# The stick-breaking loop taken by pairs of heads, with the softplus split into a high and a low half for its suffix sums

## The chip, the cores and the metric

One Trainium2 chip, one core. The time is device microseconds of one execution of the whole program. Three executions of the kernel before took 3491.86, 3499.81 and 3503.06 us. The engines are named as in the profile: PE is TensorE (PEld its weight loads), DVE is VectorE, ACT is ScalarE, POOL is GpSimd, SP is SyncE, which only issues DMAs here.

## What is computed

Sequence 512, width 1024, fp32 throughout. Two layers of a first block (`DEPTH = 2`), each with two SwiGLU feed-forwards, a mixer and a gated embedding; then a block with a sparse attention ("dsa"), and one with dilated attention ("dil"), each with a feed-forward. The mixer of the first block has three branches; this case is about the first.

```python
def stick_breaking_attention(q, k, v):          # 4 heads of 64, blocks of 128 queries
    z = einsum("bqhd,bkhd->bhqk", q[:, start:end], k[:, :end]) * scale
    mask = s_idx < t_idx                        # key before query
    log_not = where(mask, -softplus(z), 0.0)
    after = cumsum(log_not, axis=3, reverse=True) - log_not
    w = where(mask, exp(log_sigmoid(z) + after), 0.0)
    out = einsum("bhqk,bkhd->bqhd", w, v[:, :end])

def latent_attention(c_q, c_kv, ...):           # 8 heads
    q = rmsnorm(c_q, g_q) @ w_uq                # 8 pieces of weights give q, k and v of all heads
    kv = rmsnorm(c_kv, g_kv) @ w_ukv
    ...
```

## The kernel before

Everything is kept transposed: channels or keys on the 128 partitions, the 512 tokens along the free axis. Each matmul with weights is done in three: the weights are split by POOL into a high half `WH` and a low half `WL` of type fp32r, the activations likewise by ACT (`HH`) and DVE (`HL`), and PE adds high by high, low by high and high by low (L566 to L568, function `piece`). SP loads the weight pieces into a ring of slots as PE releases them (`piece_used`), POOL splits them (L490, L492), PE waits on `w_split`. Matmuls without weights take fp32 operands directly; PE runs each of them as two instructions.

Engines run their own lists in order and wait for each other by semaphores; nothing is reordered. In each of the two layers the mixer begins with `project_mix` (18 pieces), then runs `stick_breaking_and_latent_heads`, a loop over the 16 units `SB_UNITS` (4 heads by 4 blocks of keys, last block first), then `attend("mla")`.

A unit (h, b) has keys of block b in the partitions and the S - 128 b queries from that block on in the free axis, so its width is 128, 256, 384 or 512. Its steps:

- PE `z(u)`: scores by one fp32 matmul over 64 rows (L776), and the strict mask by a bf16 matmul (L777), into one of four banks of PSUM, one for each block, `psA` and `psB`.
- ACT `log1p(u)`: Abs, Exp, Ln (L1307, L1309, L1311) into `SBE`, each after the one before.
- DVE `softplus(u)`: max(z, 0) + log1p in one instruction (L1610) into `SBL`, fp32.
- PE `r(u)`: for each block k from b to 3, adds -softplus, by fp32 matmuls with a triangle (`tri`) or minus ones (`onen`) (L784), onto z in the same bank.
- ACT `weight(u)`: Exp of the bank (L1318) into `SBW`.
- PE `pv(h)`, when the four blocks of a head are there: four fp32 matmuls with 64 columns of values (L792) into half of the partitions of `psD`.

`r(u)` and `weight(u)` run `LATE = 2` units behind `z(u)`. Between the units lie the eight weight pieces of the latent attention, `latent_pieces(m)` at every second unit, 15 matmuls of 512 columns for m = 0, 1, 2, 3, 5, 7 and 6 for m = 4, 6, into `psC`. DVE scales their results (L1619 to L1624) and adds one to `mla_done`; PE waits for that before it takes `psC` again. `turn_latents(c)` rotates queries by one fp32 matmul (L820, c = 0, 1 only) and transposes four blocks of values (L823). DVE finishes the rotation, ACT copies the values (L1333).

The mean of the squares of the residual stream, needed for the scale `RS` of each normed stage, is one fp32 matmul with `onen`, `mean_square_x` (L622), which stands behind the fifth piece of the stage; ACT turns it into `RS`, and DVE needs `RS` for each projection that it takes out of PSUM.

In the "dsa" block `project_dsa` takes 18 pieces; the keys and queries of an index branch are rotated (`rotate`, L851, and `turn` on DVE, L1672 to L1675), its weights transposed (`index_weights`, L1029), and 24 logit matmuls (`logits`, L1021) feed a long top-k selection on DVE.

Of the kernel before, what the change touches and what calls it, by code (L numbers as in the profile page):

```python
# [117 lines left out]
def program(nc, A, trips):  # L118
# [86 lines left out]
    SBE = sb("SBE", [P, 3, S], offset=Yo)  # L205
    SBL = sb("SBL", [P, 10 * P], offset=Yo + 6 * KB)
    SBW = sb("SBW", [P, 10 * P], offset=Yo + 11 * KB)
# [39 lines left out]
    z_ready, zl_ready, zsp_ready, e_ready, w_ready = map(sem, ("z_ready", "zl_ready", "zsp_ready", "e_ready", "w_ready"))  # L247
# [92 lines left out]
    INDEX, MEMORY_ROUNDS = 8, 10  # L340
    logit_bank = lambda i: (PB, PC)[i % 4 // 2][:, i % 2]
# [77 lines left out]
    LATE = 2  # L419
# [132 lines left out]
    def _(pe):  # L552
# [66 lines left out]

        def mean_square_x():  # L620
            pe.wait_ge(xsum_ready, n.full(xsum_ready))
            pe.matmul(MS_X, onen, Y[:, 0], start=True, stop=True).then_inc(xms_ready, 1)  # L622

        def ffn(normed=True, embedding=False):
            if normed:
                first_four((gate_bank(0), up_bank(0), gate_bank(1), up_bank(1)))
                whole(gate_bank(2), RING)
                mean_square_x()
# [103 lines left out]
        def project_mix():  # L732

            first_four([mix_bank(p) for p in range(4)])
            whole(mix_bank(4), RING)
            mean_square_x()
# [28 lines left out]
        def stick_breaking_and_latent_heads():  # L765

            def z(u):
                h, b = SB_UNITS[u]
                r = slice(64 * (h % 2), 64 * (h % 2) + 64)
                if u >= QB:  # L770
                    pe.wait_ge(w_ready, w_base + u - QB + 1)
                elif u == 0:
                    pe.wait_ge(pj_done, n.now(pj_done) - 2)
                elif u == 2:
                    pe.wait_ge(pj_done, n.now(pj_done))
                pe.matmul(sb_bank(b), PROJ[r, C_SK + h // 2, b * P:(b + 1) * P], PROJ[r, C_SQ + h // 2, b * P:S], start=True, stop=False)  # L776
                pe.matmul(sb_bank(b)[:, 0:P], identb[:], mb[:, M_STRICT:M_STRICT + P], start=False, stop=True).then_inc(z_ready, 1)  # L777

            def r(u):
                h, b = SB_UNITS[u]  # L780
                pe.wait_ge(zsp_ready, n.full(zsp_ready))
                for k in range(b, QB):
                    o = sb_bank(b)[:, (k - b) * P:]
                    mm = pe.matmul(o, tri if k == b else onen, SBL[:, sb_at(k):sb_at(k) + sb_w(k)], start=False,  # L784
                                   stop=k == QB - 1, skip_group_check=True)
                mm.then_inc(e_ready, 1)

            def pv(h):
                pe.wait_ge(w_ready, w_base + QB * (h + 1))
                for b in range(QB):  # L790
                    o = PD[64 * (h % 2):64 * (h % 2) + 64, h // 2, b * P:S]
                    mm = pe.matmul(o, VT[:, 0, b, h * HD:(h + 1) * HD], SBW[:, sb_at(b):sb_at(b) + sb_w(b)],  # L792
                                   start=b == 0, stop=b == QB - 1, skip_group_check=True)
                mm.then_inc(sbo_ready, 1)

            def latent_pieces(m):
# [3 lines left out]
                if m > 0 and m % 2 == 0:  # L800
                    pe.wait_ge(mla_done, n.full(mla_done))
                else:
# [13 lines left out]
            def turn_latents(c):  # L816
                pe.wait_ge(mla_done, n.full(mla_done))
                if c < 2:
                    n.room(rot_done)
                    pe.matmul(PC[:, 1], cf[:, C_PMLA:C_PMLA + P], QM[:, 4 + c], start=True, stop=True).then_inc(rot_ready, 1)  # L820
                n.room(vt_done)
                for b, src in enumerate(v_list("mla")[c][0]):
                    t = pe.transpose(PC[:, 0, b * P:(b + 1) * P], src, ident)  # L823
# [1319 lines left out]
```

## Time and profile before

| | us |
|---|---|
| median of three executions | 3499.81 |
| lowest, highest | 3491.86, 3503.06 |
| the profiled execution | 3505.06 |
| its span, first to last instruction | 3503.8 |
| PE busy | 3349.5 (96%) |
| PE weight loads | 2646.4 (76%) |
| DVE busy | 1721.2 (49%) |
| ACT busy | 716.5 (20%) |
| POOL busy | 2417.6 (69%) |
| granted TensorE clock, mean | 0.982 |

An engine's busy time is the union of its instructions. Matmuls are pipelined: one lasts some 0.19 us longer than the time after which the next may start, so the cost of a matmul in a stream is the distance from start to start. A row of the timeline merges neighbours of one line; its length is from the first start to the last end.

### The profile page before, as it was taken

The page shows a single profiled execution, that of the slowest core. Times are in us where ns is not written, and L with a number is a line of the kernel's source. Part 1 is how long each engine was busy: PE and PEld are TensorE (multiplying, and loading weights), DVE is VectorE, ACT ScalarE, POOL GpSimd, SP SyncE. Part 2 cuts the span into 40 slices and gives each one's busy share as a digit, 9 for nine tenths or more (in the row PEclk, how much of TensorE's full clock was granted, in tenths as well). Part 3 has the DMA queues.
Part 4 walks back from the last instruction along what each step waited for, and adds up shares of the span by engine and source line. Part 5 has one row for each costly group of instructions (what it writes and reads, how often), then busy time and mean ns, then how long its engine had stood idle before and what let it go on. Part 6 is the DMA issues. An engine that isn't in the chain of part 4 may idle for free. (4 is left out here: it accounts for less than half of the span.)

```text
span 3503.8 us, 42241 instructions
## 1 busy us (share of the span) xinstructions
PE 3349.5 (96%) x15333; PEld 2646.4 (76%) x15333; DVE 1721.2 (49%) x1879; ACT 716.5 (20%) x1437; POOL 2417.6 (69%) x1115
## 2 busy tenths in 40 slices
PE   7999999899999999999999999897999999989998
PEld 6888775688887888776578887664688887768887
DVE  5444343454557545253464574586544324454421
ACT  2111124311114111123421113214311101231100
POOL 7888752488886888864278888561488787538875
PEclk9999999999999999999999999998999999999999
DMA  3223220122332223322022233220122222212222
GB/s 123 96 96 105 89 86 31 61 95 98 105 120 73 97 97 104 114 72 73 25 84 96 96 113 109 88 76 10 55 96 96 102 102 98 72 43 96 97 101 96
DMA packets 84369, 305.19 MB, mean 87 GB/s; under 512 B 9360, under 2 KB 9616, under 8 KB 83984
## 3 DMA queue, kind: packets, MB, share of 16 engines
q1 hardware_dynamic: 80928, 292.59, 24.1%
q10 hardware_dynamic: 3312, 10.86, 0.8%
q8 instruction: 83, 1.36, 0.2%
q14 instruction: 46, 0.38, 0.0%
HBM read 299.22 MB, written 4.19 MB: 87 GB/s over the span
## 5 line engine op out<-in xcount | busy, mean ns | idle before, releaser
L490 POOL TENSOR_TENSOR WH<-raw,scalars 128x1024 fp32r<-128x1024 f32 (+1 forms) x554 | 1043.9, 1884 | 1017.7 <-DMA raw<-in_w 944.3
L492 POOL TENSOR_TENSOR WL<-raw,WH 128x1024 fp32r<-128x1024 f32 (+1 forms) x554 | 1370.7, 2474 | 43.5
L566 PE MATMUL psA<-HH,WH 128*128 128x512 f32 x1136 | 455.1, 401 | 2.2 <-DVE PROJ L1786 2.2
L568 PE MATMUL psA<-HL,WH 128*128 128x512 f32 x1136 | 444.1, 391 | 0.0
L567 PE MATMUL psA<-HH,WL 128*128 128x512 f32 x1136 | 444.0, 391 | 0.0
L566 PE MATMUL psC<-HIDH,WH 128*128 128x512 f32 x1056 | 416.1, 394 | 0.0
L568 PE MATMUL psC<-HIDL,WH 128*128 128x512 f32 x1056 | 414.0, 392 | 0.0
L567 PE MATMUL psC<-HIDH,WL 128*128 128x512 f32 x1056 | 409.8, 388 | 0.0
L566 PE MATMUL psC<-HH,WH 128*128 128x512 f32 x832 | 325.9, 392 | 3.8 <-DVE HL L1645 3.8
L567 PE MATMUL psC<-HH,WL 128*128 128x512 f32 x832 | 324.1, 390 | 0.0
L568 PE MATMUL psC<-HL,WH 128*128 128x512 f32 x832 | 324.1, 390 | 0.0
L1554 DVE TENSOR_TENSOR HIDL<-Y,HIDH 128x512 f32 (+1 forms) x132 | 248.3, 1881 | 125.7 <-ACT HIDH L1211 125.7
L566 PE MATMUL psB<-HH,WH 128*128 128x512 f32 x696 | 272.3, 391 | 0.0
L567 PE MATMUL psB<-HH,WL 128*128 128x512 f32 x696 | 271.5, 390 | 0.0
L568 PE MATMUL psB<-HL,WH 128*128 128x512 f32 x696 | 271.3, 390 | 0.0
L1552 DVE TENSOR_TENSOR Y<-Y 128x512 f32<-128x512 f32 x132 | 250.5, 1898 | 22.1 <-DVE Y L1549 9.6
L566 PEld LDWEIGHTS psA<-HH,WH 128*128 128x128 f32 x1136 | 214.0, 188 | 56.4 <-issue 9.1
L567 PEld LDWEIGHTS psA<-HH,WL 128*128 128x128 f32 x1136 | 214.1, 188 | 49.5 <-issue 5.5
L568 PEld LDWEIGHTS psA<-HL,WH 128*128 128x128 f32 x1136 | 214.1, 188 | 45.5
L1211 ACT ACTIVATE HIDH<-Y 128x512 f32 x132 | 83.5, 632 | 789.0 <-DVE Y L1552 789.0
L568 PEld LDWEIGHTS psC<-HIDL,WH 128*128 128x128 f32 x1056 | 198.2, 188 | 46.4
L567 PEld LDWEIGHTS psC<-HIDH,WL 128*128 128x128 f32 x1056 | 198.2, 188 | 44.4
(347 smaller groups left out, 4708.1 us busy)
## 6 DMA issues: line engine op xcount, KB each, us to landing
raw<-in_w SPq DMA_DIRECT2D x554, 512.0 KB, 3.2
X<-in_x ACTq DMA_DIRECT2D x4, 512.0 KB, 9.1
NRAW<-in_mem ACTq DMA_DIRECT2D x2, 1024.0 KB, 5.2
out<-Y SPq DMA_DIRECT2D x8, 256.0 KB, 2.2
POSI<-in_pos ACTq DMA_DIRECT2D x4, 256.0 KB, 2.6
PRAW<-in_p ACTq DMA_DIRECT2D x2, 512.0 KB, 3.5
table_F<-newF ACTq DMA_DIRECT2D x2, 512.0 KB, 2.6
table_I<-newI ACTq DMA_DIRECT2D x2, 512.0 KB, 3.8
```

The lines of the kernel that those rows point to most:

```text
L490: pool.tensor_tensor(WH[j][:, 0:w], raw[j][:, 0:w], zero[:, 0:1].broadcast_to([P, w]), ALU.subtract).then_inc(w_hi, 1)
L492: pool.tensor_tensor(WL[j][:, 0:w], raw[j][:, 0:w], WH[j][:, 0:w], ALU.subtract).then_inc(w_split, 1)
L566: pe.matmul(out, WH[slot][:, w], hi[:, t], start=start and t == 0, stop=False)
L567: pe.matmul(out, WL[slot][:, w], hi[:, t], start=False, stop=False)
L568: mm = pe.matmul(out, WH[slot][:, w], lo[:, t], start=False, stop=stop and t == tiles - 1)
L1211: act.activation(HIDH[:, bass.ds(2 * i + j, 1)].rearrange("p a n -> p (a n)"), US[:, j], ACT.Copy).then_inc(hidh_ready, 1)
L1552: dve.tensor_tensor(US[:, j], US[:, j], GS[:, j], ALU.mult).then_inc(hf_ready, 1)
L1554: dve.tensor_tensor(HIDL[:, at].rearrange("p a n -> p (a n)"), US[:, j], HIDH[:, at].rearrange("p a n -> p (a n)"), ALU.subtract).then_inc ...
```

## The change

The loop goes over 8 pairs (`SB_PAIRS`: two heads, one block of keys) instead of 16 units. `z(u)` issues the scores of both heads of a pair one behind the other, rows 0 to 63 and rows 64 to 127; `pv(c)` does two heads alternately, into partitions 0 to 63 and 64 to 127. The banks of PSUM go by pair, two pairs at a time. The softplus is now written in fp32 over `SBE` (DVE), copied to fp32r `SBLH` (ACT, `high`), and the rest subtracted into fp32r `SBLL` (DVE, `low`); `r(i)` does two fp32r matmuls, one with each half, where one fp32 matmul stood. The order of PE, ACT and DVE in the loop is rewritten; the ACT copies and DVE subtractions of the convolution (`HH[:, 6 + c]`, `HL[:, 6 + c]`) move behind the loop. The latent values are transposed into `psD` instead of `psC`, and the rotation goes there too.

Outside the loop: the mean-square matmul stands in the middle of the fifth piece instead of behind it, in the normed stages; and `project_dsa` orders the rotations, the transposition of the index weights and the first logits anew.

```diff
-    SB_UNITS = [(h, b) for h in range(SBH) for b in reversed(range(QB))]
+    SB_PAIRS = [(c, b) for c in range(2) for b in reversed(range(QB))]
+    SB_UNITS = [(c, b, x) for c, b in SB_PAIRS for x in range(2)]
-    sb_bank = lambda b: (PA, PA, PB, PB)[b][:, b % 2, 0:S - b * P]
+    sb_bank = lambda i: (PB, PA)[i // 2 % 2][:, i % 2, 0:sb_w(SB_UNITS[i][1])]
+    latent_value_bank = lambda c: PD[:, c // 2]
...
+        def whole_around_mean_square(out, slot):
+            pe.wait_ge(w_split, n.full(w_split))
+            piece(slot, out, HH, HL, KD // 2, stop=False, done=None)
+            mean_square_x()
+            piece(slot, out, HH[:, KD // 2:], HL[:, KD // 2:], KD // 2, start=False, first_tile=KD // 2)
...
             def z(u):
-                if u >= QB:
-                    pe.wait_ge(w_ready, w_base + u - QB + 1)
+                if u >= 2:
+                    pe.wait_ge(w_ready, w_base + 2 * u - 2)
...
+                for x in range(2):
+                    r = slice(64 * x, 64 * x + 64)
+                    pe.matmul(sb_bank(2 * u + x), PROJ[r, C_SK + c, b * P:(b + 1) * P], PROJ[r, C_SQ + c, b * P:S], start=True, stop=False)
+                for x in range(2):
+                    pe.matmul(sb_bank(2 * u + x)[:, 0:P], identb[:], mb[:, M_STRICT:M_STRICT + P], start=False, stop=True).then_inc(z_ready, 1)
+
+            def r(i):
+                c, b, x = SB_UNITS[i]
                 pe.wait_ge(zsp_ready, n.full(zsp_ready))
                 for k in range(b, QB):
...
+                    w = ones_r[:, 0:P] if k == b else ones_r[:, P:2 * P]
+                    pe.matmul(o, w, SBLH[:, x, at], start=False, stop=False, skip_group_check=True)
+                    mm = pe.matmul(o, w, SBLL[:, x, at], start=False, stop=k == QB - 1, skip_group_check=True)
...
             def latent_pieces(m):
...
+                elif m % 2 == 0:
+                    pe.wait_ge(mla_done, n.full(mla_done))
...
             def turn_latents(c):
                 pe.wait_ge(mla_done, n.full(mla_done))
+                pe.wait_ge(rot_done, n.now(rot_done))
...
-            for u in range(len(SB_UNITS) + LATE):
-                if u < len(SB_UNITS):
+            for u in range(len(SB_PAIRS) + 1):
+                if u < 2:
                     z(u)
-                if u % 2 == 1 and u // 2 < MH:
-                    latent_pieces(u // 2)
-                if u >= LATE:
-                    r(u - LATE)
-                if u % 4 == 2 and u < 16:
-                    turn_latents(u // 4)
-                if u >= LATE + 1 and (u - LATE) % QB == 0:
-                    pv((u - LATE) // QB - 1)
-            pv(SBH - 1)
+                if u < MH:
+                    latent_pieces(u)
+                if 2 <= u < len(SB_PAIRS):
+                    z(u)
+                if u == QB + 1:
+                    pv(0)
+                if u >= 1:
+                    r(2 * u - 2)
+                    r(2 * u - 1)
+                if u % 2 == 0 and u < MH:
+                    turn_latents(u // 2)
+            pv(1)
...
         def stick_breaking():        # ACT
...
+            for u in range(len(SB_PAIRS) + 1):
+                units, older = ((2 * u, 2 * u + 1) if u < len(SB_PAIRS) else (), (2 * u - 2, 2 * u - 1) if u > 0 else ())
+                for i in units:
+                    log1p(i)
+                if u == QB:
+                    for i in older:
+                        weight(i)
+                    for i in units:
+                        high(i)
+                else:
+                    for x in range(2):
+                        if units:
+                            high(units[x])
+                        if older:
+                            weight(older[x])
...
         def stick_breaking_and_latent_heads():        # DVE
+            for u in range(len(SB_PAIRS)):
+                softplus(2 * u)
+                softplus(2 * u + 1)
+                low(2 * u)
+                latent_pieces(u)
+                low(2 * u + 1)
+                if u in (0, 2):
+                    turn([(QM[:, 4 + u // 2], P, tabM, C_PMLA)], PD[:, 1])
             for c in range(2):
                 low_of(PD[:, c], c)
+            for c in range(2):
+                low_of(T[:, c], 6 + c)
...
             ropes = rope_list("idx")        # PE, project_dsa
-            for p in (6, 7):
-                next_piece(p)
-                memory_squares(2 * (p - 6))
-                memory_squares(2 * (p - 6) + 1)
-                rotate(*((ropes[:3], 0) if p == 6 else (ropes[3:], 1)))
+            pe.wait_ge(pj_done, n.now(pj_done))
+            rotate(ropes[:2])
+            index_weights()
+            next_piece(6, ((5, lambda: rotate(ropes[2:3])),))
+            rotate(ropes[3:4], 1)
+            memory_squares(0)
+            memory_squares(1)
+            next_piece(7, ((5, lambda: rotate(ropes[4:])),))
+            memory_squares(2)
+            memory_squares(3)
+            pe.wait_ge(vt_done, n.now(vt_done))
+            logits(0)
```

## Rows read from the trace of the kernel before

**Rows 1.** Windows view, the loop of layer 0: busy of each engine, clock, DMA.

```profile
501.54:573.76 72.22, 69.87 (x285) 44.52 (x284) 24.87 (x41) 31.71 (x70) 31.83 (x19) 1.00 0.20 66
```

**Rows 2.** Timeline view, PE in the loop: start us, length us, instructions [idle before].

```profile
502.12 0.70 PE L776 MATMUL psB<-PROJ 64*128 64x256 f32 x2
...
507.86 1.13 PE L820 MATMUL psC<-QM,cf 128*128 128x512 f32 x2
508.82 0.60 PE L823 MATMUL psC<-cf,PROJ 128*128 128x128 f32 x4
509.35 1.12 PE L776 MATMUL psA<-PROJ 64*128 64x512 f32 x2
...
521.70 2.32 PE L784 MATMUL psA<-SBL,cf 128*128 128x512 f32 x8
...
571.39 2.37 PE L792 MATMUL psD<-SBW,VT 128*64 128x512 f32 x8 [0.69 <-ACT SBW L1318]
```

**Rows 3.** Timeline view, PE in the memory attention, where two heads already alternate.

```profile
2400.22 0.70 PE L933 MATMUL psB<-KVM,PROJ 64*128 64x256 f32 x4
...
2401.44 0.66 PE L966 MATMUL psD<-PRTb,VMEMa 128*64 128x128 f32 x8
```

**Rows 4.** Timeline view, fp32r matmuls of 512 and of 256 columns.

```profile
500.09 0.39 PE L566 MATMUL psA<-HH,WH 128*128 128x512 f32 x1
500.32 0.39 PE L567 MATMUL psA<-HH,WL 128*128 128x512 f32 x1
...
2357.06 0.28 PE L567 MATMUL psA<-NH,WL 128*128 128x256 f32 x1
...
2359.10 0.28 PE L567 MATMUL psA<-NH,WL 128*128 128x256 f32 x1
```

**Rows 5.** Timeline view, ACT in the loop.

```profile
502.23 0.28 ACT L1307 ACTIVATE SBE<-psB 128x128 f32<-128x128 f32 x1 [10.84 <-PE psB L777]
...
503.09 0.36 ACT L1307 ACTIVATE SBE<-psB 128x256 f32<-128x256 f32 x1
...
510.70 0.60 ACT L1307 ACTIVATE SBE<-psA 128x512 f32<-128x512 f32 x1
...
511.99 0.63 ACT L1311 ACTIVATE SBE<-SBE 128x512 f32<-128x512 f32 x1
```

**Rows 6.** Timeline view, DVE takes a latent piece out of PSUM.

```profile
515.03 0.69 DVE L1619 TENSOR_TENSOR QM<-psC,RY 128x512 f32<-128x512 f32 x1 [0.35 <-PE psC L568]
515.64 0.68 DVE L1620 TENSOR_TENSOR PROJ<-psC,YSS 128x512 f32<-128x512 f32 x1
```

**Rows 7.** Source view, L1645 on DVE: duration ns min/median/max, first and last start.

```profile
L1645 DVE TENSOR_TENSOR HL<-T,HH x4: 680/1374/2068, 511.4 to 1605.6; 128x512 fp32r<-128x512 f32 x4
```

**Rows 8.** Timeline view, POOL in the loop.

```profile
511.50 2.03 POOL L492 TENSOR_TENSOR WL<-raw,WH 128x640 fp32r<-128x640 f32 x1
```

**Rows 9.** Windows view, PE around idle times: busy of each engine, clock, DMA.

```profile
387.00:390.00 3.00, 0.08 (x1) 0.00 (x0) 1.43 (x2) 1.24 (x2) 3.00 (x2) 0.93 0.96 362
396.00:399.00 3.00, 3.00 (x8) 2.31 (x7) 2.93 (x5) 1.69 (x3) 0.00 (x0) 0.50 0.00 0
2380.00:2400.00 20.00, 11.97 (x56) 7.07 (x56) 18.99 (x57) 7.42 (x27) 0.00 (x0) 0.50 0.00 1
```

**Rows 10.** Timeline view, ACT behind the loop.

```profile
573.80 1.08 ACT L1337 ACTIVATE HH<-psD 128x512 fp32r<-128x512 f32 x2 [2.46 <-PE psD L792]
```

**Rows 11.** Timeline view, a mean square: the last sum on DVE, its matmul on PE.

```profile
1512.43 0.69 DVE L1502 TENSOR_TENSOR Y<-Y 128x512 f32<-128x512 f32 x1
...
1517.00 1.02 PE L622 MATMUL psD<-Y,cf 128*128 128x512 f32 x2
```

**Rows 12.** Timeline view, PE in the projection of the dsa block.

```profile
2258.80 1.13 PE L851 MATMUL psC<-PROJ,cf 128*128 128x512 f32 x2 [2.95 <-DVE PROJ L1675]
...
2276.50 0.66 PE L1029 MATMUL psC<-cf,PROJ 128*128 128x128 f32 x4 [4.32 <-DVE PROJ L1675]
```

**Rows 13.** Windows view, the same stretch and the selection that follows it.

```profile
2252.00:2282.00 30.00, 22.58 (x77) 15.00 (x76) 16.23 (x19) 4.02 (x11) 10.78 (x5) 0.89 0.10 35
2340.00:2360.00 20.00, 17.27 (x98) 14.66 (x96) 19.66 (x49) 0.00 (x0) 18.06 (x9) 1.00 0.31 106
```

More of the change, by code:

```diff
@@ L1311, in log1p, with high, weight @@
                 act.activation(e, e, ACT.Ln, bias=1.0).then_inc(zl_ready, 1)
-            def weight(u):
-                h, b = SB_UNITS[u]
+            def high(i):
+                act.wait_ge(za_ready, n.full(za_ready))
+                act.activation(SBLH[:, i % 2, sb_part(i)], sb_exp(i), ACT.Copy).then_inc(zh_ready, 1)
+            def weight(i):
                 act.wait_ge(e_ready, n.full(e_ready))
-                if u >= QB and u % QB == 0:
+                if i == 2 * QB:
                     act.wait_ge(sbo_ready, n.full(sbo_ready))
-                act.activation(SBW[:, sb_at(b):sb_at(b) + sb_w(b)], sb_bank(b), ACT.Exp).then_inc(w_ready, 1)
@@ L1320, in stick_breaking @@
-            sp_base = n.now(zsp_ready)
-            for u in range(len(SB_UNITS) + LATE):
-                if u < len(SB_UNITS):
-                    log1p(u)
-                if u == 2:
-                    act.wait_ge(pj_done, n.now(pj_done))
-                    for c in range(2):
-                        act.wait_ge(cv_ready, n.full(cv_ready))
-                        act.activation(HH[:, 6 + c], T[:, c], ACT.Copy).then_inc(oh_ready, 1)
-                if u >= LATE:
-                    weight(u - LATE)
-                if u % 4 == 2 and u < 16:
+                act.activation(SBW[:, i % 2, sb_part(i)], sb_bank(i), ACT.Exp).then_inc(w_ready, 1)
@@ new lines, in stick_breaking @@
+            act.wait_ge(pj_done, n.now(pj_done) - 2)
+            for u in range(len(SB_PAIRS) + 1):
[7 more added lines that the diff above has]
+                        high(i)
+                else:
+                    for x in range(2):
+                        if units:
+                            high(units[x])
+                        if older:
+                            weight(older[x])
+                if u % 2 == 0 and u < MH:
@@ L1337, in stick_breaking @@
                 act.activation(HH[:, c], PD[:, c], ACT.Copy).then_inc(oh_ready, 1)
+            for c in range(2):
+                act.wait_ge(cv_ready, n.full(cv_ready))
+                act.activation(HH[:, 6 + c], T[:, c], ACT.Copy).then_inc(oh_ready, 1)
         def attend(which):
@@ L1604, in stick_breaking_and_latent_heads, with softplus, low @@
         def stick_breaking_and_latent_heads():
-            def softplus(u):
-                h, b = SB_UNITS[u]
+            def softplus(i):
                 dve.wait_ge(zl_ready, n.full(zl_ready))
-                if u >= QB and u % QB == 0:
-                    dve.wait_ge(e_ready, e_base + u)
-                dve.scalar_tensor_tensor(out=SBL[:, sb_at(b):sb_at(b) + sb_w(b)], in0=sb_bank(b), scalar=0.0,
-                                         in1=SBE[:, u % 3, 0:sb_w(b)], op0=ALU.max, op1=ALU.add).then_inc(zsp_ready, 1)
+                dve.scalar_tensor_tensor(out=sb_exp(i), in0=sb_bank(i), scalar=0.0, in1=sb_exp(i),
+                                         op0=ALU.max, op1=ALU.add).then_inc(za_ready, 1)
+            def low(i):
+                dve.wait_ge(zh_ready, n.full(zh_ready))
+                dve.tensor_tensor(SBLL[:, i % 2, sb_part(i)], sb_exp(i), SBLH[:, i % 2, sb_part(i)], ALU.subtract).then_inc(zsp_ready, 1)
             def latent_pieces(m):
@@ L1626, in latent_pieces @@
                 n.full(mla_done)
-            e_base = n.now(e_ready)
-            for u in range(len(SB_UNITS) + 1):
-                if u in (2, 6):
-                    turn([(QM[:, 4 + u // 4], P, tabM, C_PMLA)], PC[:, 1])
-                if u < len(SB_UNITS):
-                    softplus(u)
-                if u == 2:
-                    for c in range(2):
-                        low_of(T[:, c], 6 + c)
-                if u % 2 == 1:
-                    latent_pieces(u // 2)
-            n.full(e_ready, len(SB_UNITS))
+            for u in range(len(SB_PAIRS)):
[6 more added lines that the diff above has]
+                    turn([(QM[:, 4 + u // 2], P, tabM, C_PMLA)], PD[:, 1])
             for c in range(2):
                 low_of(PD[:, c], c)
+            for c in range(2):
+                low_of(T[:, c], 6 + c)
         def low_of(src, c, which="mla"):
```

110 lines of the change are left out of this document (50 added, 60 removed).

## The prediction

> **What bounds the kernel now.** The page first: PE is busy 96% of the span, all others 69% or less, so a change pays only where PE does less or waits less. Then the windows view over the loop of layer 0 [rows 1]: it lasts 72.2 us, PE is busy 69.9 of them at clock 1.00, DVE 24.9, ACT 31.7, POOL 31.8. PE bounds the loop too, with some 2.3 us of waits. Layer 1 has the same loop. All of this holds because PE's list mixes short units finely enough that ACT and DVE always finish one while PE has another; the question is what the new order does to that.
>
> **PE's own work shrinks.** Four parts, each by distances from start to start.
>
> *Scores.* A unit of 256 columns is 0.70 us long [rows 2]. In the memory attention two heads of 256 columns, on different halves of the rows, take four instructions in the same 0.70 us [rows 3]. So a pair costs what one unit cost. A unit of 512 is 1.12 us; with the mask matmul and less the overlap the four widths need 3.4 us a head. Four heads cost 13.6 before, two pairs 6.8: -6.8 us a layer.
>
> *Values.* `pv` of one head is 2.37 us, 2.3 from start to start [rows 2]. Alternating heads with half the columns of the array run side by side as well: eight instructions of 128 columns in 0.66 us [rows 3], where four transposes of the same size take 0.60 [rows 2]. Four runs become two: -4.6 us.
>
> *Suffix sums.* The widest unit has 1280 columns in eight fp32 instructions, 2.2 us [rows 2], 1.7 ns a column. An fp32r matmul costs 0.23 us at 512 columns and 0.113 at 256 (18 of them in 2.04 us) [rows 4]; it is issued twice. For 128 columns the trace has no fp32r row: by columns it would be 0.06, by the nearest row 0.113. I take 0.11, because the weights loaded for it are the same 128 columns. A head with one 512, two 384, three 256 and four 128 then needs 2.7 us instead of 4.4: -6.8 us a layer (-8.4 with 0.06).
>
> *Waits* of 2.3 us could go as well. Were the loop still PE's, it would last about 54 us.
>
> **But the order of the lists makes a chain of it.** From pair 2 on PE issues the latent pieces of step u, then z(u), then the sums of pair u-1, and then needs `mla_done` of step u: at even u in `turn_latents`, at odd u ahead of the next pieces. DVE gives `mla_done` only after `softplus(2u)`, `softplus(2u+1)` and `low(2u)`, which wait for z(u) through six ACT operations and the copy `high(2u)`. Behind PE's wait stand all later pieces and z(u+1), and behind that ACT. So one step is: scores, six ACT operations, the last softplus (the copy hides beside it), `low`, the scaling of the pieces, the turning if there is one, the next pieces, next scores. Before, a unit had three ACT operations, and its DVE work lay in front of no PE wait that long.
>
> The prices. Scores until ACT starts: 0.7 us at 128 columns to 1.3 at 512 (the 1.12 and the mask) [rows 2]. Three ACT operations take 0.86 us from start to start at 128 columns [rows 5], and 1.92 at 512 (510.70 to 512.62) [rows 5]; twice that is 1.75 and 3.85, with 2.4 and 3.1 between. Softplus reads PSUM as the scaling does: 0.69 at 512 [rows 6]. `low` reads two tiles of SBUF and writes fp32r, as L1645 on T does: 0.68 us, or 2.07 beside POOL's split [rows 7, 8]. At 512 columns I take the middle, 1.4, less at smaller widths, because POOL is at work 44% of the loop. The scaling is 1.29 us, with its hand-over 1.4, and 0.8 for steps 4 and 6 [rows 6]. Turning costs 1.5 us with the rotation (507.86 to 509.35) and 0.6 without [rows 2]. 15 pieces of 0.227 are 3.5 us with the entry, six are 1.5 [rows 4].
>
> From scores to scores: step 0 is 0.6 + 3.5 + 1.5 + 1.5 = 7.1. Step 1, 0.9 + 3.5 + 1.4 + 3.5 = 9.3. Step 2, 1.1 + 3.1 + 0.6 + 1.1 + 1.4 + 1.5 + 3.5 = 12.3. Step 3, 1.3 + 3.85 + 0.7 + 1.4 + 1.4 + 1.5 = 10.1. Step 4 waits for the sums of the widest pair, because the high halves of the new heads take the old ones' place: 0.7 + 2.5 + 0.7 + 0.3 + 0.3 + 0.8 + 0.6 + 3.5 = 9.4. Step 5, 0.9 + 2.4 + 0.45 + 0.75 + 1.4 + 1.5 = 7.4. Step 6, 1.1 + 3.1 + 0.6 + 1.1 + 0.8 + 0.6 + 3.5 = 10.8. From z(7) to the end, 1.3 + 3.85 + 0.7 + 1.4 + 1.4, the other `low` 0.7, its sums 1.25, its weight 0.7, `pv(1)` 2.3: 13.6. The loop is 80 us, 77 with every `low` free of POOL and 83 with none: 7.8 us longer than before, with some 25 us of idle PE where there were 2.3.
>
> At this place the Trainium skill (TensorEngine Tiling (Array Packing), PSUM Bottleneck) warns that tiling speeds TensorE up while the emptying of PSUM stays and may become the bound. By TensorE alone the loop is the 54 us above, by this warning it is nearer the 80.
>
> **The clock.** The idle stretches of PE are 12.3 - 1.1 - 0.9 - 1.5 - 3.5 = 5.3 us in step 2, 5.8 in step 3, 4.7 in step 6, and 4 at the end. In the trace PE did 0.08 us of work from 387 to 390; later it ran at 0.50, eight matmuls in 3.0 us where 13 fit at full clock, and in the memory attention, busy 60%, it stayed at 0.50 for 20 us [rows 4, 9]. That is 1.2 GHz instead of 2.4. PE work behind the four gaps that the chain waits for is 6.2, 2.7, 5.2 and 3.6 us, 18 in all. All of it at half clock costs 18 us, none costs 0; I take 7, since long runs of pieces follow and each stretch would end within them. The Trainium skill (TensorE: Matmul & The Clock Gate, Part 1) holds that the throttled state is the default and activity lifts it; the rows agree, and by it some loss is to be expected rather than none.
>
> **Behind the loop.** ACT copied two chunks for `attend` in 1.08 us [rows 10]; now it copies four, and DVE's subtractions follow them, ahead of the first peak: +1.1 us a layer. Inside the loop the removed copies were hidden.
>
> **Outside.** The mean-square matmul comes 12 matmuls, 2.7 us, earlier. The tightest of the seven instances that move had its sum ready at 1513.12 and its matmul at 1517.00 [rows 11], so no wait arises; no PE wait follows a later scale either, so nothing is won: 0, hidden by the rest of the pieces. Without that cover the cost would be the missing part of 2.7 us, seven times.
>
> The dsa projection is different. PE waited 2.95 and 4.32 us there [rows 12], and the clock was 0.89 over 30 us, that is 6.6 us at half, a loss of 3.3 [rows 13]. The new order puts piece 6 or 7 behind each rotation. It adds a wait for the sixth chunk's scaling, 0.8 us. In all -9.8. Does it reach the end? The selection behind it is DVE's, 19.66 of 20 us [rows 13], but DVE starts on it just as much earlier. I take -9, bounds -5 and -10, once.
>
> **Sum.** Two layers of 7.8 + 7 + 1.1 = 15.9 are 31.8; less 9 is +23 us. The profiled execution took 3505.1, 1.3 of it outside the span and 5.3 above the median; 3528 on its base is 3523 on the median's.
>
> **Rivals.**
> - *PE stays the bound* and the change does what its parts promise: 2 x (54 - 72.2 + 1) - 9 = -43, 3457 us. For it speaks that every PE part shrinks by measured rows; against it, that nothing in the new lists lets PE run ahead of `mla_done`. It decides if the DVE order leaves less than 5 us of idle per step. 12%.
> - *The chain, but no loss of clock.* 2 x 8.9 - 9 = +9, 3509 us, within or just above the bound of no change. The mean clock of 1.00 over the old loop [rows 1] speaks for it, the four gaps against. 18%.
> - *Half clock through both loops*, as in the memory attention [rows 9]. Pieces, scores, turning and sums on the chain, about 38 us, double: 2 x (7.8 + 38 + 1) - 9 = +85, 3585 us. Against it: 3.5 us of dense pieces in most steps. 12%.
> - *The forecast*, chain and part of the clock: 3510 to 3545. 55%, the rest scattered.
>
> The range of 8 in 10, 3490 to 3565, leaves out the first rival and most of the third. About 0.3% can be told from no change. Faster gets the first rival and a little more, 0.14; same most of the second, 0.18; slower 0.68.
>
> **What would show it.** The loop's window: 85 to 90 us instead of 72.2, PE busy under 75%. PE waits of 4 to 6 us, released by DVE L1619 to L1624's successors (`QM`, `PROJ` out of `psC`), four a layer. The clock below 1.00 in it. The pair of scores at 512 columns: 1.1 us for four instructions. `low` at 512: 0.7 to 2.1 us. In dsa no waits of 3 and 4 us. The prediction is wrong if PE waits for `mla_done` are under 2 us, which would mean that DVE reached the scaling earlier than I read, or if the clock falls for longer than the gaps.

## The result, and the profile after

| | us |
|---|---|
| before, median of four executions | 3495.84 |
| after, median of four executions | 3535.6 |
| after, lowest and highest | 3530.6, 3546.38 |
| ratio after to before, 95% interval | 1.0119 (1.0099 to 1.014) |
| span of the profiled execution after | 3538.9 |

The change makes the kernel 1.2% slower: 42 us by the ratio, 40 us by the two medians. The forecast was 23 us slower, 3523 us. The page of the profile after: span, busy time of each engine, and the granted clock in 40 slices.

```profile
span 3538.9 us, 42276 instructions
PE 3344.4 (95%) x15333; PEld 2653.3 (75%) x15333; DVE 1742.5 (49%) x1911; ACT 726.5 (21%) x1471; POOL 2418.5 (68%) x1115
...
PEclk9999997999999999999899999998999999999999
```

PE's busy time has hardly changed, from 3349.5 to 3344.4 us, although two loops should need 18 us less each. The clock digits show where this went: the 7 is the slice from 531 to 619 us, which holds most of the first loop, and the first 8 the slice from 1681 to 1769 us, with the end of the second loop and the `attend` behind it. (The other 8, from 2389 us on, is the memory attention and stands in the page of before too.) The windows view over the loop of each layer answers [rows 1]; below them come the stretches of the first loop in which the clock was low and PE worked (columns: window, length; busy us of PE, PEld, DVE, ACT, POOL; clock, DMA share, GB/s).

```profile
500.25:594.83 94.58, 66.65 (x284) 46.65 (x283) 39.51 (x55) 35.32 (x84) 32.77 (x19) 0.80 0.15 50
...
1619.30:1711.30 92.00, 62.54 (x285) 44.46 (x285) 39.20 (x55) 35.41 (x84) 32.12 (x19) 0.83 0.16 52
...
523.51:529.59 6.08, 6.08 (x14) 4.23 (x15) 2.46 (x4) 0.60 (x1) 0.07 (x1) 0.50 0.01 3
539.66:543.24 3.58, 3.58 (x10) 2.32 (x10) 0.47 (x1) 0.00 (x0) 0.00 (x0) 0.50 0.00 0
550.07:553.48 3.41, 3.41 (x10) 2.63 (x9) 0.32 (x1) 0.00 (x0) 0.17 (x1) 0.50 0.00 0
561.38:567.14 5.76, 5.76 (x17) 3.65 (x18) 1.17 (x1) 0.96 (x2) 0.88 (x1) 0.50 0.27 89
570.94:573.96 3.02, 3.02 (x9) 2.56 (x10) 1.98 (x1) 0.60 (x1) 1.57 (x1) 0.50 0.02 5
584.96:594.44 9.48, 8.72 (x28) 5.89 (x30) 1.74 (x3) 1.19 (x2) 0.00 (x0) 0.50 0.00 0
```

The loop lasts 94.6 and 92.0 us where it lasted 72.2, and 28 of the 94.6 us are idle PE. The timeline of PE shows the idle times and what ended them. A row with L787 is a z, the start of a step; L838 is the rotation, L842 the transposition of values, L572 the first matmul of latent pieces, L798 a sum with a high half, L808 `pv`.

```profile
500.25 0.49 PE L787 MATMUL psB<-PROJ 64*128 64x128 f32 x4
505.84 1.13 PE L838 MATMUL psD<-QM,cf 128*128 128x512 f32 x2 [1.38 <-DVE PROJ L1658]
...
507.34 0.70 PE L787 MATMUL psA<-PROJ 64*128 64x256 f32 x4
...
513.28 0.50 PE L572 MATMUL psC<-CH,WH 128*128 128x512 f32 x1 [1.13 <-DVE PROJ L1654]
516.92 0.92 PE L787 MATMUL psB<-PROJ 64*128 64x384 f32 x4
...
523.51 2.07 PE L838 MATMUL psD<-QM,cf 128*128 128x512 f32 x2 [4.53 <-DVE PROJ L1658]
...
531.34 1.13 PE L787 MATMUL psA<-PROJ 64*128 64x512 f32 x4
...
539.66 0.79 PE L572 MATMUL psC<-CH,WH 128*128 128x512 f32 x1 [5.36 <-DVE PROJ L1654]
542.52 0.80 PE L787 MATMUL psB<-PROJ 64*128 64x128 f32 x4
...
548.77 0.65 PE L842 MATMUL psD<-cf,PROJ 128*128 128x128 f32 x4 [2.68 <-DVE PROJ L1658]
554.39 0.70 PE L787 MATMUL psA<-PROJ 64*128 64x256 f32 x4
...
561.38 0.79 PE L572 MATMUL psC<-CH,WH 128*128 128x512 f32 x1 [3.17 <-DVE PROJ L1654]
564.23 1.65 PE L787 MATMUL psB<-PROJ 64*128 64x384 f32 x4
...
570.94 1.11 PE L842 MATMUL psD<-cf,PROJ 128*128 128x128 f32 x4 [3.32 <-DVE PROJ L1658]
576.40 1.13 PE L787 MATMUL psA<-PROJ 64*128 64x512 f32 x4
...
584.96 0.79 PE L798 MATMUL psA<-SBLH,ones_r 128*128 128x512 f32 x1 [5.59 <-DVE SBLL L1645]
```

Each step has its idle time, and from step 0 to step 6 the releaser is the scaling of a latent piece (L1654, L1658), the operation that gives `mla_done`. The timeline of DVE in step 3 shows why it comes so late:

```profile
534.62 0.69 DVE L1640 SCALAR_TENSOR_TENSOR SBE<-psA,SBE 128x512 f32<-128x512 f32 x1 [6.99 <-ACT SBE L1332]
536.43 0.69 DVE L1640 SCALAR_TENSOR_TENSOR SBE<-psA,SBE 128x512 f32<-128x512 f32 x1 [1.12 <-ACT SBE L1332]
537.04 1.30 DVE L1645 TENSOR_TENSOR SBLL<-SBE,SBLH 128x512 fp32r<-128x512 f32 x1
538.26 0.68 DVE L1653 TENSOR_TENSOR QM<-psC,RY 128x512 f32<-128x512 f32 x1
538.86 0.68 DVE L1654 TENSOR_TENSOR PROJ<-psC,YSS 128x512 f32<-128x512 f32 x1
```

DVE stands idle for 6.99 us, and for the last 3.2 of them the latent results lie ready in `psC`: PE's last matmul of the pieces ends at 531.4. The first operation in DVE's list is the softplus of a score that PE issued only at 531.34. Then follow both softpluses and one `low`, and only then the two scalings that PE needs, the first at 538.26, 6.9 us after its input was ready.

The difference by stages, from the timelines of the two profiled executions (`attend`: from its first score to its last). "Before, second" is another profile of the kernel before; it tells how much a stage differs by itself.

| us | before | before, second | after | after less before |
|---|---|---|---|---|
| loop, layer 0 | 72.2 | 72.2 | 94.6 | +22.4 |
| loop, layer 1 | 72.1 | 72.2 | 91.9 | +19.8 |
| `attend`, layer 0 | 48.5 | 45.5 | 51.5 | +3.0 |
| `attend`, layer 1 | 47.1 | 45.5 | 51.4 | +4.3 |
| end of `attend` to the first dsa logit | 566.5 | 558.0 | 550.6 | -15.9 |
| logits | 33.3 | 33.2 | 35.0 | +1.7 |
| all other stages | 2664.1 | 2661.7 | 2663.9 | -0.2 |
| span | 3503.8 | 3488.3 | 3538.9 | +35.1 |

### The profile page after: what moved, and what is told of

Same layout as the page of the kernel before. It is cut to its first block and busy times, and to the rows that moved or that the text cites. A ratio compares the mean times of both kernels' runs of the same rounds, so it can differ in the third digit from the quotient of the medians.

```text
span 3538.9 us, 42276 instructions
## 1 busy us (share of the span) xinstructions
PE 3344.4 (95%) x15333; PEld 2653.3 (75%) x15333; DVE 1742.5 (49%) x1911; ACT 726.5 (21%) x1471; POOL 2418.5 (68%) x1115
## 5 line engine op out<-in xcount | busy, mean ns | idle before, releaser
L572 PE MATMUL psA<-HH,WH 128*128 128x512 f32 x1136 | 455.1, 401 | 2.2 <-DVE PROJ L1818 2.2
L572 PE MATMUL psC<-HIDH,WH 128*128 128x512 f32 x1056 | 416.1, 394 | 0.0
L572 PE MATMUL psC<-HH,WH 128*128 128x512 f32 x832 | 325.9, 392 | 3.8 <-DVE HL L1677 3.8
L1587 DVE TENSOR_TENSOR HIDL<-Y,HIDH 128x512 f32 (+1 forms) x132 | 257.5, 1950 | 126.2 <-ACT HIDH L1235 126.2
L572 PE MATMUL psB<-HH,WH 128*128 128x512 f32 x696 | 272.3, 391 | 0.0
L572 PEld LDWEIGHTS psA<-HH,WH 128*128 128x128 f32 x1136 | 213.6, 188 | 57.3 <-issue 10.2
```

Of the source, the lines that this page charges most:

```text
L572: pe.matmul(out, WH[slot][:, w], hi[:, t], start=start and t == 0, stop=False)
L1587: dve.tensor_tensor(HIDL[:, at].rearrange("p a n -> p (a n)"), US[:, j], HIDH[:, at].rearrange("p a n -> p (a n)"), ALU.subtract).then_inc ...
```

## The experiments

Each kernel was timed beside the kernel before on the same chip; a ratio is to that kernel, with its 95% interval; 1% is 35 us. The kernel before took 3490.5 us on one of these chips and 3498 to 3499 us on two others, so ratios are compared and not absolute times.

**Is it the order of DVE's list?** The changed kernel, with the two softpluses put behind the latent scaling. PE, ACT and the halves stay.

```diff
             for u in range(len(SB_PAIRS)):        # DVE
-                softplus(2 * u)
-                softplus(2 * u + 1)
-                low(2 * u)
-                latent_pieces(u)
-                low(2 * u + 1)
+                if u < 2:
+                    softplus(2 * u)
...
+                else:
+                    latent_pieces(u)
+                    softplus(2 * u)
+                    softplus(2 * u + 1)
+                    low(2 * u)
+                    low(2 * u + 1)
```

> The changed kernel with one edit: from pair 2 on DVE scales the latent pieces of a step before its softpluses and low halves, not between them. Theory (the chain): PE no longer waits behind z(u), the ACT operations and the low half for mla_done, so the waits of 4.5, 5.4, 2.7, 3.2 and 3.3 us that stand in the changed kernel's loop ahead of the turning or the pieces go; what is left is PE's own work or ACT's ten operations a step. Step by step 7.1 + 9.3 + 7.0 + 7.5 + 7.3 + 5.1 + 6.2 + 12.2 = 62 us for the loop instead of 94.6, little or no half clock in it, and about 3465 us in all, below the kernel before too. Rival (ACT and DVE are simply too slow for pairs, whatever the order): the waits only move to the scores, which wait for the weights; the loop stays above 80 us, 3505 us or more.

Measured: 3486.79 us against 3490.51, ratio 0.999 (0.9976 to 1.0003). The loops last 67.0 and 65.0 us. PE's waits in the first of them (engine and line that waited, releaser: us in total, times, longest):

```profile
PE psA L798 <- DVE SBLL L1645: 4.9, 1, 4.9
PE psC L572 <- DVE PROJ L1654: 1.7, 2, 1.1
PE psB L787 <- ACT SBW L1342: 1.7, 1, 1.7
PE psD L838 <- DVE PROJ L1658: 1.4, 1, 1.4
```

In the changed kernel the first two releasers by size were PROJ L1654 with 9.7 us and L1658 with 11.9. Swapping five calls in one engine's list takes back 27 us a layer and 0.0129 of the ratio, 45 us: the whole slowdown, since 0.999 can't be told from the kernel before. The chain through `mla_done` is shown. The expected 3465 us were missed by 22 us. From z to z the first seven steps take 47.7 us, where 49.5 were expected; the last takes 18.5 us where 12.2 were expected, as long as in the changed kernel. There PE needs the last pair's `low` with nothing else to do, 4.9 us, and runs at half clock behind it, which the expectation had put at little or nothing. `attend` also stays at 51.5 and 51.4 us, and the dsa stage gives less than its 9 us (below).

**What do the halves cost?** The changed kernel, with the softplus in one fp32 tensor and the old fp32 sums; no copy `high`, no subtraction `low`.

```diff
-                    pe.matmul(o, w, SBLH[:, x, at], start=False, stop=False, skip_group_check=True)
-                    mm = pe.matmul(o, w, SBLL[:, x, at], start=False, stop=k == QB - 1, skip_group_check=True)
+                    mm = pe.matmul(o, tri if k == b else onen, SBL[:, x, at], start=False, stop=k == QB - 1, skip_group_check=True)
```

> The changed kernel without the two halves: softplus goes straight to an fp32 tile, the suffix sums are one fp32 matmul each again, and the high copy on ACT and the subtraction on DVE are left out. Theory (the chain sets the loop, PE is idle anyway): each of steps 2 to 7 loses the low half, 0.7 to 1.4 us, from its chain; the sums grow by 6.8 us a layer, but most of that falls into idle PE, only the last pair's (+0.9 each of two) and the widest pair's in step 4 (+1.9) are on the chain. Loop some 3 to 5 us shorter than 94.6, 3525 to 3530 us in all. Rival (PE's work sets the loop): 6.8 us a layer are added, 3549 us.

Measured: 3507.1 us, ratio 1.0043 (1.0029 to 1.0058); loops of 79.2 and 77.9 us.

```profile
499.20:578.40 79.20, 63.63 (x283) 42.35 (x282) 22.32 (x39) 29.49 (x68) 32.04 (x19) 0.94 0.18 60
```

The split was to save PE 6.8 us a layer. Inside this chain it costs 15.4 and 14.0. The expectation, loops of some 90 to 92 us, was over 10 us a loop too high. The chain without `low` is shorter, and PE has longer sums in its gaps, so the idle times are 3.63, 3.11, 1.42, 1.27 and 2.95 us instead of 4.53, 5.36, 2.68, 3.17 and 3.32, and the clock is 0.94 over the loop instead of 0.80, which the expectation had left out. How much is the one and how much the other these rows don't separate.

**What does the clock cost?** The changed kernel with its order, and additional fp32 matmuls of 512 columns on constants in steps 2 to 7, placed ahead of PE's wait. They write a bank that is free then, and nothing reads them.

```diff
+            FILL = {2: 4, 3: 5, 4: 2, 5: 3, 6: 3, 7: 5}
+                if u in FILL:
+                    pe.wait_ge(rot_done, n.now(rot_done))
+                    pe.wait_ge(vt_done, n.now(vt_done))
+                    for _ in range(FILL[u]):
+                        pe.matmul(PD[:, 1], onen, tabM[:, 0], start=True, stop=True)
```

> The changed kernel with fp32 matmuls of 512 columns that nobody reads put into PE's idle stretches: 4, 5, 2, 3, 3 and 5 of them in steps 2 to 7, 0.86 us each at full clock, so that each ends before what PE waits for. Theory (half of the excess is the clock): the clock stays at 1.00 through the loop, the loop falls from 94.6 to 80 us, which is the chain by itself, and attend starts at full clock; 29 us less in the loops and some 4 behind them, 3500 to 3508 us. Rival (the chain alone is about 90 us and the clock costs little): the loop stays at 88 us or more, 3525 us or more.

Measured: 3516.09 us, ratio 1.0077 (1.005 to 1.0105). The two loops, then the head of the first `attend`, and the fillers of one step:

```profile
499.00:581.20 82.20, 71.64 (x327) 45.00 (x326) 39.53 (x55) 35.30 (x84) 32.94 (x19) 1.00 0.18 58
1605.21:1688.51 83.30, 71.94 (x328) 44.90 (x327) 41.67 (x55) 35.33 (x84) 32.46 (x19) 1.00 0.18 57
586.30:603.40 17.10, 17.02 (x68) 7.81 (x66) 6.48 (x17) 6.17 (x22) 0.00 (x0) 0.50 0.00 0
...
530.48 4.51 PE L837 MATMUL psD<-tabM,cf 128*128 128x512 f32 x10
```

With more work for PE the loops are shorter: 82.2 and 83.3 us (from the first score to the end of the last `pv`) instead of 94.6 and 91.9. The clock is 1.00 throughout. So the chain alone is at most 82 us (behind the filler of step 5 PE did not wait any more, so there it may be a little long), and the clock's part is 12.4 and 8.6 us. The time came out 8 us above the expected 3500 to 3508 us: the loops 2 to 3 us each, and the `attend` behind them did not get faster as expected. It lasts 53.0 and 52.7 us, with 17.1 us at half clock that begin behind a wait of its own, 1.85 us at its third scores.

**The dsa projection alone.** The kernel before with the new order of `project_dsa` and nothing else. The core of the edit:

```diff
-            for p in (6, 7):
-                next_piece(p)
-                ...
-                rotate(*((ropes[:3], 0) if p == 6 else (ropes[3:], 1)))
+            pe.wait_ge(pj_done, n.now(pj_done))
+            rotate(ropes[:2])
+            index_weights()
+            next_piece(6, ((5, lambda: rotate(ropes[2:3])),))
+            rotate(ropes[3:4], 1)
+            ...
+            next_piece(7, ((5, lambda: rotate(ropes[4:])),))
```

> The kernel before with the new order of the dsa projection alone (PE, DVE, and the index weights in another bank). By the prediction -9 us, that is 3487 us beside 3496: the waits of 2.95 and 4.32 us go, and the clock stays up there. In the changed kernel the first logits came 11.9 us earlier after the stage's start, but the stages behind gave back 2 us. Rival (the selection on DVE ends at its own time, or the clock falls for longer later): under 4 us are left.

Measured: 3486.74 us against 3490.51, ratio 0.999 (0.998 to 1.0001), 3.8 us less by the medians; the interval reaches from 7 us less to nothing. The stretch that [rows 13] shows, as far from the first logit in this kernel as there, and PE's two waits in it:

```profile
2226.80:2256.80 30.00, 27.97 (x113) 19.52 (x112) 16.66 (x24) 5.93 (x15) 18.96 (x10) 1.00 0.31 106
...
2234.29 1.98 PE L852 MATMUL psC<-PROJ,cf 128*128 128x512 f32 x4 [0.78 <-DVE PROJ L1791]
...
2255.66 0.70 PE L1022 MATMUL psB<-PROJ 64*128 64x256 f32 x4 [1.10 <-ACT WIT L1440]
```

The waits of 3 and 4 us are gone, the added one is 0.78 us where 0.8 was forecast, and the clock is 1.00, yet the gain is less than half of -9. A second profile of the kernel before gives part of the reason:

> The kernel before once more, for a second profile of it. If the clock's falls at fixed points of the program make its time, the same stretches are at half clock as in the first profile and the stages last the same within 1 us. If they depend on the moment, single stages differ by 2 to 4 us, which is then the noise under which a difference of one stage between two profiles can't be read.

It took 3489.64 us. The same stretch, again counted from the first logit, and the same two waits as in [rows 12]:

```profile
2240.15:2270.15 30.00, 26.46 (x108) 18.52 (x107) 15.46 (x21) 4.74 (x13) 19.00 (x9) 1.00 0.23 86
...
2252.29 1.13 PE L851 MATMUL psC<-PROJ,cf 128*128 128x512 f32 x2 [1.24 <-DVE PROJ L1675]
...
2266.21 0.66 PE L1029 MATMUL psC<-cf,PROJ 128*128 128x128 f32 x4 [2.15 <-DVE PROJ L1675]
```

In this execution the waits are 1.24 and 2.15 us instead of 2.95 and 4.32, and the clock doesn't fall. From one profile to the other the stage differs by 8.5 us. The forecast took the waits of one execution for the kernel's. Against the second profile the stage and the logits gain 7.4 - 1.8 = 5.6 us, which agrees with the 3.8 measured. But the slow form isn't rare: the profile of the mean-square kernel below, which has the old order here, shows 2.96 and 4.18 us and 566.7 us for the stage, so it stands in two of three profiles, while all eight with the new order have 550.4 to 550.7 us. By those two the gain would be 14 us. On the chip of this run the kernel before took 3490.5 us, near the profile with the short waits (3489.6 us); that it mostly ran in that form there would fit, but isn't shown.

**The mean square alone.** The kernel before with the mean-square matmul in the middle of the fifth piece.

```diff
-                whole(gate_bank(2), RING)
-                mean_square_x()
+                whole_around_mean_square(gate_bank(2), RING)
```

> The kernel before with the mean-square matmul in the middle of the fifth piece, and nothing else. The prediction put it at nothing: its sum is ready in time, and no PE wait follows a later scale. 3490 us, ratio 0.999 to 1.001. Rival (the earlier scale lets DVE take the first projections sooner and something behind gains): 3 us or more.

Measured: 3497.66 us, ratio 1.0003 (0.9989 to 1.0017). Nothing, as forecast.

**The head of `attend`.** The first experiment's kernel, with the convolution's two copies and two subtractions moved from ahead of `attend` into its first steps.

```diff
-            for c in range(2):
-                act.wait_ge(cv_ready, n.full(cv_ready))
-                act.activation(HH[:, 6 + c], T[:, c], ACT.Copy).then_inc(oh_ready, 1)
...
+                if which == "mla" and j in (0, 1):        # ACT, behind the exponentials of pair j
+                    act.wait_ge(cv_ready, n.full(cv_ready))
+                    act.activation(HH[:, 6 + j], T[:, j], ACT.Copy).then_inc(oh_ready, 1)
...
+                if which == "mla" and j in (1, 2):        # DVE, behind the normalization of pair j - 1
+                    low_of(T[:, j - 1], 5 + j)
```

> The run with the scaling first, and one more edit: the two ACT copies and two DVE subtractions of the convolution leave the place between the loop and the attention and stand inside the first steps of the attention. Theory (they delay the first peak and exponential, PE runs out of work, and the clock falls on top of it): the attention of the latent heads, 51.5 us in both layers there and in the changed kernel against 48.5 and 47.1 before, goes back to 47 to 49 us; 6 to 8 us in all, about 3480 us. Rival (the attention is slow because PE has come out of an idle tail at half clock): it stays at 51 us, 3486 us.

Measured: 3482.74 us against 3499.45, ratio 0.9954 (0.9928 to 0.9981). `attend` of layer 0 at clock 1.00:

```profile
569.50:615.10 45.60, 41.73 (x328) 22.67 (x325) 25.70 (x63) 26.98 (x84) 0.00 (x0) 1.00 0.01 1
```

That is 5.9 us less than with the copies in front, though the loop ahead of it is 1.8 us longer in this profile (68.8). In layer 1 `attend` stayed at 51.8 us, with half clock from 1661.3 to 1678.4, although its wait at the third scores had gone down to 0.65 us there. So one layer bears the reason out and one doesn't; the difference in the ratio is 0.0036 with intervals of 0.0014 and 0.0027 on either side. The slowdown itself is plain: the ten `attend`s in the five profiles with the new loop and the copies in front last 51.4 to 53.4 us, the eight in the four profiles with the old loop 45.5 to 48.5.

**Both mended, and one fp32 tensor.** The first experiment's order with the fp32 sums of the second.

> Scaling first and fp32 sums together: what the two halves are worth once the chain is gone. Theory (in the mended loop some steps are ACT's and some PE's): the fp32 sums add 6.8 us of PE work a layer, the halves cost ACT 7 us and DVE 8 us; the loop stays within 2 us of the 67.0 and 65.0 us with halves, with less half clock at its end since PE has more to do; 3480 to 3490 us. Rival (with the chain gone PE is the bound): 6 us more a layer, 3499 us.

Measured: 3481.74 us against 3499.45, ratio 0.9958 (0.9941 to 0.9974).

```profile
499.40:561.10 61.70, 58.04 (x285) 39.15 (x284) 23.58 (x39) 29.18 (x68) 32.20 (x19) 1.00 0.23 77
...
567.20:580.80 13.60, 13.52 (x60) 6.80 (x58) 6.42 (x16) 5.66 (x20) 0.00 (x0) 0.50 0.01 1
```

Both loops last 61.7 us, with PE busy 94% at full clock: PE is the bound again. The halves cost 5.3 and 3.3 us even in the better order. The expectation, within 2 us of 67.0 and 65.0, missed that. From z to z the first seven steps are 2.4 us longer than with halves, 50.1 instead of 47.7, and the last is 11.7 instead of 18.5: with halves PE waits 4.9 us there for the last `low` and then runs at half clock, in this kernel it begins the same sums without a wait and at full clock. Only `attend`, with a wait of 1.85 us at its third scores and 13.6 us at half clock, holds on to 51.7 us.

**All three edits.** Order, fp32 sums, and the convolution's copies inside `attend`.

> The changed kernel with three edits together: VectorE writes the two softplus operations after the latents' copies from the third pair on, the softplus stays one fp32 tensor instead of two halves, and the two copies of the convolution's output with their subtractions go into the first steps of the attend. Nothing is left out. With the first two edits alone the loop measured 61.7 us in each layer, the attend 51.7 and 51.8 us, with a wait of 1.85 us at its third scores and 13.6 us at half clock; the ratio to the kernel before was 0.9958. If the head of the attend is what the two copies of ScalarE cost, the loops stay at 61.7 us, the wait of 1.85 us goes, and the attend comes to between 45.6 and 50 us a layer: 3 to 12 us in all below 3481.7 us, 3470 to 3479 us, a ratio of 0.992 to 0.995. The rival: the wait is not the copies' but the clock's, which falls at the wait for the last head's product whatever follows it (5 us idle ahead of it); then the attend stays at 50 to 52 us and the time within 2 us of 3481.7 us.

Measured: 3469.15 us against 3498.02, ratio 0.9917 (0.9901 to 0.9934), the fastest of all, 0.8% under the kernel before. The loop, and the third scores of `attend`:

```profile
501.71:563.46 61.75, 58.09 (x284) 39.18 (x283) 23.58 (x39) 29.17 (x68) 32.31 (x19) 1.00 0.24 77
...
566.72 1.76 PE L952 MATMUL psA<-PROJ,QM 64*128 64x384 f32 x8 [0.65 <-ACT PR L1374]
```

The loops last 61.7 us, the wait fell from 1.85 to 0.65 us where it was expected to go, and `attend` lasts 48.9 and 47.5 us, as expected. The clock still falls in it, but later and for half as long, from 574.0 to 580.8 in layer 0, around another wait, of 1.41 us at 574.17. So with the copies moved, four `attend`s in two profiles last 45.5, 51.8, 48.9 and 47.5 us: three of them as short as with the old loop or nearly so, one not. By the trace the edit gives 2.9 + 4.4 = 7.3 us; the ratios of this and the run before it give 14, with 8 on either side.

## Why the prediction was right, and where its sizes were off

**PE's own parts** came out as priced. A pair of scores at 512 columns is four instructions in 1.13 us, `pv` of two heads sixteen in 2.37. (The 54 us of the first rival leave the 2.3 us of waits in; without them it is 52.) Of the sums of the widest pair the timeline has these rows, the first and the last two of one head and the first of the other:

```profile
543.34 0.48 PE L798 MATMUL psA<-SBLH,ones_r 128*128 128x512 f32 x1
...
544.47 0.22 PE L798 MATMUL psA<-SBLH,ones_r 128*128 128x128 f32 x1
544.53 0.28 PE L799 MATMUL psA<-SBLL,ones_r 128*128 128x128 f32 x1
544.65 0.45 PE L798 MATMUL psA<-SBLH,ones_r 128*128 128x512 f32 x1
```

A head is 1.3 us, 543.34 to 544.65, instead of 2.2. From start to start a 128-column matmul costs 0.06 us with the high half and 0.11 or 0.12 with the low half, so the pair lies between the two prices that were weighed. None of this reached the end, as the forecast said.

**The chain** is right in its place and its mechanism, and its length came out within a few us. Step by step in layer 0, measured from z to z. The column at full clock is an estimate: it takes off what half clock cost on the chain, half of the stretches in the windows above as far as PE's work lay on it. The last column is measured, in the run with the gaps filled:

| step | forecast | measured | at half clock on the chain | at full clock | gaps filled |
|---|---|---|---|---|---|
| 0 | 7.1 | 7.1 | 0 | 7.1 | 7.1 |
| 1 | 9.3 | 9.6 | 0 | 9.6 | 10.1 |
| 2 | 12.3 | 14.4 | 6.1 | 11.4 | 11.5 |
| 3 | 10.1 | 11.2 | 2.9 | 9.7 | 10.0 |
| 4 | 9.4 | 11.9 | 0.7 + 3.4 | 9.8 | 10.4 |
| 5 | 7.4 | 9.8 | 2.9 | 8.4 | 7.8 |
| 6 | 10.8 | 12.2 | 1.7 + 3.0 | 9.8 | 10.6 |
| 7 to the end | 13.6 | 18.4 | 8.7 | 14.0 | 14.8 |
| sum | 80.0 | 94.6 | | 79.8 | 82.2 |

80 us were forecast, 79.8 come out of the rows, and with the gaps filled 82.2 and 83.3 were measured. Single steps are off by up to 1 us in both directions, so the agreement of the sums to 0.2 us is luck. `low` is where single terms went wrong: the ones on the chain in steps 2 to 7 took 0.55, 1.30, 0.99, 1.94, 0.55 and 2.80 us where 1.1, 1.4, 0.3, 0.75, 1.1 and 1.4 were assumed, 8.1 us instead of 6.1. The forecast took the middle of two prices by width; the last section shows what the time went by. The warning about the emptying of PSUM that stands beside the 80 does not describe this loop: DVE was busy 39.5 of 94.6 us, and what held PE up was the order of its list.

**The clock** is the term that was mis-sized: 7 us a layer forecast, 12.4 and 8.6 measured with the filled gaps, 14.8 by the table in layer 0. The forecast placed four gaps with work behind them; there were six stretches at half clock, because 2.68, 3.17 and 3.32 us of idle in steps 4 to 6 were followed by one each, of which the forecast had counted only step 6. And behind the last gap the sums and `pv(1)`, 8.7 us at half, are all on the chain; the forecast had assumed that each stretch would end within the work behind its gap. The bounds, 0 to 18, held it. One of the forecast's own signs of being wrong did come: the clock fell for longer than the gaps, 31 us of stretches against 24.7 us of gaps in layer 0.

The Trainium skill (TensorE: Matmul & The Clock Gate, Part 1) says that activity lifts the throttle. The filled gaps agree in the plainest way: 22 matmuls a layer that nobody reads made the program faster.

**Behind the loop** 1.1 us a layer was the two copies only. Measured are +3.0 and +4.3 against one profile of before and +6.0 and +5.9 against the other. With the copies in front PE waits 1.86 us at the third scores, where it waits 0.65 in the kernels that moved them and 0.64 in the kernel before, and behind that the clock falls. The wait itself is 1.2 us, near the forecast; the rest is the clock, and that it hangs on this wait is only in part shown, since in one `attend` of four it fell for 17.1 us without it. Moving them gave 5.9 us in one layer, and 2.9 and 4.4 in the version with fp32 sums. The forecast priced the operation and not what followed from it.

**Outside.** The mean square at 0 is confirmed. The dsa term, -9 with bounds of -5 and -10, measured -3.8, between -7 and nothing: too large. Waits and clock of one execution were taken for the kernel's; as two of three profiles show them, this explains only part, and the rest stays open.

**The sum.** Forecast: 2 x (7.8 + 7 + 1.1) - 9 = +23. With the measured terms: loops 22.4 + 19.8, `attend` between 7 and 12, dsa -4, together 45 to 50 us, at the upper edge of what was measured, 42 with 7 on either side. The loops were forecast 12.6 us too short, `attend` 5 to 10 and the dsa stage 5. All three errors lie on the same side, so the prediction was right in sign and mechanism and 19 us low. That the sum of the loop came out at 80 hid errors in its terms; the clock and `attend` had nothing to hide theirs.

**The rivals.** PE as the bound is refuted in this kernel: PE was busy 70% of the loop. The condition set for it, under 5 us of idle a step, was badly chosen, for in layer 0 it was met in all steps but 3 and 7 (5.36 and 5.59 us). In the two mended kernels it is what happens: the rival's 54 us of PE work become 61.7 with fp32 sums, and there the bound is PE. The chain without the clock's loss is the filled kernel, 3516 us, where 3509 had been worked out. Half clock throughout is refuted by means of 0.80 and 0.83.

**The other signs.** The loop lasted 94.6 and 91.9 us instead of 85 to 90. Waits of 4 to 6 us were three in layer 0 and four in layer 1 instead of four each, and the last of each was for `low` and not for the scaling. `low` at 512 columns took up to 2.80 us instead of 2.1.

## What to carry to other kernels

When work is moved in an engine's list, look at what the first waiting operation holds up behind it: here results lay ready for 7 us behind a softplus whose input didn't exist yet, and exchanging the two was worth 1.3% of the program. A split that saves the bounding engine time but adds an operation each to two others pays only where these aren't between that engine and its next work; so price it on the chain, not on the engine. And price a gap of PE twice, once as idle time and once as the slow work behind it, above all where that work is the end of a stage.

## What the runs showed of the hardware

- Gaps of 2.68, 3.17 and 3.32 us in PE's work, in a loop where PE is busy 70%, were each followed by 3 to 6 us of work at half clock; those of 1.13 and 1.38 us at its start were not. Layer 1 is alike: 3.17 us was followed by half clock, 2.01 us was not. In `attend`, with short matmuls, the clock fell behind shorter ones: a wait of 1.85 us was followed by 13.6 us at half clock, one of 0.65 us by 17.1 us in one layer and by none in the other.
- `low`, a subtraction of two tiles in SBUF, took from 0.29 to 2.80 us over its 32 instances, and not by width alone. With no POOL instruction beside it, 512 columns took 0.68 us. Beside one, these rows show a difference by which of the two began first:

```profile
569.74 0.55 DVE L1645 TENSOR_TENSOR SBLL<-SBE,SBLH 128x384 fp32r<-128x384 f32 x1
569.79 2.71 POOL L498 TENSOR_TENSOR WL<-raw,WH 128x1024 fp32r<-128x1024 f32 x1
...
582.01 2.35 POOL L498 TENSOR_TENSOR WL<-raw,WH 128x1024 fp32r<-128x1024 f32 x1
582.10 2.80 DVE L1645 TENSOR_TENSOR SBLL<-SBE,SBLH 128x512 fp32r<-128x512 f32 x1
```

  At 569.74 `low` began first and was not slowed; POOL's subtraction took 2.71 us instead of 2.35. At 582.10 it began 0.09 us behind POOL's and ended 0.54 us after it, as if it had waited for it to end. The one of 1.30 us at 537.04 ended 0.55 us after a POOL subtraction (536.25 to 537.79) in the same way. So the price of `low` goes by the moment at which it meets POOL, and the 1.4 us of the forecast was a mean of two cases.
- Two profiled executions of one kernel differ in single stages by up to 8.5 us, where the clock falls in one and not in the other. A stage's difference of a few us between two profiles is no result unless the timed runs bear it out.
